# Two attention stages change places between two fences, in a hybrid encoder layer on one core

## What is computed

```python
x = x + 0.5 * SwiGLU_1(RMSNorm(x))                 # w1_gate, w1_up, w1_down; width 2816
z = RMSNorm(x) @ w_in                              # q, k, v of both groups, indexer q, k, w
# group A: differential attention, 4 heads, q/k split in two 64-wide halves
p = softmax(q1 k1) - lam * softmax(q2 k2);  o = RMSNorm(p @ v) * (1 - lam_init)
# group B (DSA): 8 heads, one shared key and value; a 4-head indexer picks
# k = min(256, L // 4) admissible keys per query, and only these are attended
x = x + concat(A, B) @ w_out
x = x + 0.5 * SwiGLU_2(RMSNorm(x))
```

## Time and profile before

| | |
|---|---|
| Timed runs | 2506.95, 2510.47, 2513.23 us; median 2510.47 |
| Profiled execution | 2504.2 us, span 2502.4 us |
| TensorE busy | 2435.7 us, 97% of the span |
| VectorE, ScalarE, GpSimd busy | 1441.7, 1044.7, 268.3 us |
| Mean granted TensorE clock | 0.995 |
| Main pieces beside the two attentions | lines 1403 to 1405 and 1420 to 1422 |

### The profile page before, as it was taken

How to read it: one execution, slowest core, us unless ns; L and a number is a source line. 1 busy time by engine, 2 the same in 40 slices (tenths; PEclk the granted TensorE clock), 3 DMA queues, 4 the chain that set the end, 5 groups by cost and what they waited for, 6 DMA issues and landing times.

```text
span 2502.4 us, 36218 instructions
## 1 busy us (share of the span) xinstructions
PE 2435.7 (97%) x13547; PEld 2104.8 (84%) x13547; DVE 1441.7 (58%) x2875; ACT 1044.7 (42%) x1811; POOL 268.3 (11%) x364
## 2 busy tenths in 40 slices
PE   7999999999999999998899999999999999999998
PEld 7999999978877678777788988999979889888887
DVE  5544444464257458887544468888875635444444
ACT  4322222233234346656433457876555533222221
POOL 1100000014210001110013200000100001000000
PEclk9999999999999999999899999999999999999999
DMA  6212121233357353333424542322321132322331
GB/s 234 81 68 85 68 85 68 85 134 110 122 163 247 113 158 123 100 115 88 175 68 148 166 146 72 101 87 73 94 61 51 37 144 84 133 93 86 102 101 67
DMA packets 169323, 271.28 MB, mean 108 GB/s; under 512 B 72032, under 2 KB 104832, under 8 KB 169152
## 3 DMA queue, kind: packets, MB, share of 16 engines
q0 software_dynamic: 43200, 167.29, 19.8%
q1 hardware_dynamic: 125952, 101.68, 12.8%
HBM read 235.21 MB, written 35.29 MB: 108 GB/s over the span
## 4 chain that ended last, share of the span: by engine, by line
PE 88%; DVE 4%; issue 3%; DMA 2%; ACT 1%; SPq 1%; DVEq 0%; POOL 0%; ACTq 0%
PE bank L1403 14%; PE bank L1405 14%; PE bank L1404 14%; PE bank L1420 7%; PE bank L1421 7%; PE bank L1422 7%; PE bank L1440 5%; PE bank L1442 5%; PE bank L1441 5%; PE bank L1532 3%; PE bank L1501 2%; PE bank L1502 1%; PE bank L1515 1%; PE bank L1460 1%; DMA rows<-o_scr 1%
## 5 line engine op out<-in xcount | busy, mean ns | idle before, releaser
L1993 DVE TENSOR_TENSOR w_lo<-raw,w_hi 128x1024 fp32r<-128x1024 f32 x320 | 385.9, 1216 | 135.4 <-ACT w_hi L1707 134.9
L1403 PE MATMUL bank<-XTh_a,w_hi 128*128 128x320 f32 x1408 | 440.4, 313 | 2.8 <-DVE w_lo L1993 2.5
L1405 PE MATMUL bank<-XTh_a,w_lo 128*128 128x320 f32 x1408 | 436.1, 310 | 0.0
L1404 PE MATMUL bank<-XTl_a,w_hi 128*128 128x320 f32 x1408 | 436.0, 310 | 0.0
L1707 ACT ACTIVATE w_hi<-raw 128x1024 fp32r<-128x1024 f32 x320 | 332.0, 1047 | 217.3 <-PE bank L1442 127.5
L1420 PE MATMUL bank<-w_hi,hid_hi 128*128 128x512 f32 x792 | 317.9, 401 | 10.9 <-DVE X_a L2024 5.4
L1421 PE MATMUL bank<-w_lo,hid_hi 128*128 128x512 f32 x792 | 312.6, 395 | 0.0
L1422 PE MATMUL bank<-w_hi,hid_lo 128*128 128x512 f32 x792 | 310.4, 392 | 0.0
L1403 PE MATMUL bank<-XTh_b,w_hi 128*128 128x512 f32 x704 | 282.8, 402 | 0.0
L2024 DVE SCALAR_TENSOR_TENSOR X_a<-bank,X_a 128x512 f32<-128x512 f32 x220 | 151.1, 689 | 224.2 <-PE bank L1422 223.5
L1404 PE MATMUL bank<-XTl_b,w_hi 128*128 128x512 f32 x704 | 278.3, 395 | 0.0
(11 more groups left out here) (326 smaller groups left out, 3954.6 us busy)
## 6 DMA issues: line engine op xcount, KB each, us to landing
raw<-in_w_gate POOLq DMA_DIRECT2D x44, 1024.0 KB, 5.6
raw<-in_w_up POOLq DMA_DIRECT2D x44, 1024.0 KB, 5.7
raw<-in_w_down POOLq DMA_DIRECT2D x44, 1024.0 KB, 5.2
raw<-in_w_in POOLq DMA_DIRECT2D x16, 1024.0 KB, 5.4
s_k_in<-in_cache_diff_k SPq DMA_DIRECT2D x16, 512.0 KB, 4.5
s_v_in<-in_cache_diff_v SPq DMA_DIRECT2D x8, 1024.0 KB, 5.9
raw<-in_w_out POOLq DMA_DIRECT2D x8, 1024.0 KB, 5.5
q_rows_b<-q_scr SPq DMA_DIRECT2D x80, 64.0 KB, 2.0
```

Source lines behind the costliest of these rows:

```text
L1403: pe.matmul(out, hi[:, k], XTh[g][:, k, lo:up], start=(k == 0), stop=False)
L1404: pe.matmul(out, hi[:, k], XTl[g][:, k, lo:up], start=False, stop=False)
L1405: last = pe.matmul(out, low[:, k], XTh[g][:, k, lo:up], start=False, stop=(k == KD - 1))
L1993: dve.tensor_tensor(hilo(w_lo, u)[:, :, 0:width_of(u)], raw_part(u), hilo(w_hi, u)[:, :, 0:width_of(u)].bitcast(F32), ALU.subtract).then_i ...
```

## The change

The two attentions of the side list change places, and `fence` with them: `enter` of GA (1) now lets the prompt's attention start, a plain raising behind `leave` (2, `past_attention`) lets the sample's start, and `past_sample` keeps its wait for the sample's stores, stands behind the sample and raises nothing. The numbers that `opened`, `near_zero` and `x_begin` wait for, and the planner's needs, are turned round to match.

```diff
@@ needs
         if kind in ("k_load", "q_load", "near", "values"):
-            return [("fence",), ("enter", GB)]
+            return [("enter", GA), ("enter", GB)]
@@
         if kind in ("x_q", "x_tables"):
-            return [("x_begin",), ("enter", GA)] + ([("x_tables",)] if kind == "x_q" else [])
+            return [("x_begin",), ("fence",)] + ([("x_tables",)] if kind == "x_q" else [])
@@ att_items
-    out += [("opened", 2 if g == GA else 3), ("k_split", g, 0), ("k_low", g, 0)]
+    out += [("opened", 1 if g == GA else 3), ("k_split", g, 0), ("k_low", g, 0)]
@@ sample_items
-    out += [("opened", 1), ("x_tables",), ("x_q", "dq"), ("x_q", "iq"), ("x_q", "w"), ("x_key", "i", 0),
+    out += [("opened", 2), ("x_tables",), ("x_q", "dq"), ("x_q", "iq"), ("x_q", "w"), ("x_key", "i", 0),
@@ make_plan
-    plan += merge(s.take(), [("enter", GA)] + sample_items() + [("fence",)] + att_items(GA)
+    plan += merge(s.take(), [("enter", GA)] + att_items(GA) + [("fence",)] + sample_items() + [("past_sample",)]
                   + [("reload", GA)] + out_items("ota", 5), pace=PACE[GA])
@@ gpsimd
                 def near_zero(g):
-                    pool.wait_ge(fence, 2 if g == GA else 3)
+                    pool.wait_ge(fence, 1 if g == GA else 3)
@@
                 def x_begin():
-                    pool.wait_ge(fence, 1)
+                    pool.wait_ge(fence, 2)
@@ sync
                 def past_sample():
                     sp.wait_ge(s_stored, 32)
+
+                def past_attention():
                     sp.sem_inc(fence, 1)
@@
-                          "fence": past_sample}
+                          "fence": past_attention, "past_sample": past_sample}
```

## The result

The changed kernel takes 2519.97 us (median of twelve runs, 2515.23 to 2523.98), the kernel before 2509.80 beside it (2505.87 to 2513.23). The ratio is 1.0043 with a 95% interval of 1.0035 to 1.0050: 10 us slower. That lies inside the forecast's range (2503 to 2526), but not at its likeliest case: +2.4 us was said, and a time over 2518 had a chance of 0.23.

What follows compares the result with a forecast made beforehand. TensorE was taken as the bound, busy 2435.7 of 2502.4 us, so only idle gaps or slow-clock stretches could change. Start 0, middle +0.5 and end +1.9 summed to +2.4 us: median 2510.47 to 2512.9, range 2503 to 2526.

Steps and rivals of the forecast that it cites:

- Start, 0: Start of the prompt's attention, now first: its loads land before the planner's some 14 pieces end; cost 0.
- Middle, +0.5: Joint from prompt's attention to sample: loads need 10.2 us against 9.7 covered by about 5 pieces; 0.5 us, bounds 0 to 4.3.
- The stages' own draw unchanged: Attention stages: each uses as many of the 217 feed-forward pieces as before; only the three joints change.
- End, stand: Sample to projection: rows ready 14.5 us after `x_end`, 4 pieces cover 5.6; TensorE stands 8.9 us at first output transpose.
- The 2.3 us of the hidden-layer chain: Tail, ahead of line 1420: this wait for the last pair goes, as the chain runs during the stand.
- End, row waits gone: Tail, third and fifth tile: the 3.0 us of row waits go, covered by four pieces behind the first transposes.
- End, clock: Tail: one slow-clock stretch losing 1.7 us follows the stand, where two of 1.7 each were lost before.
- The stock runs out: Rival: stages draw more, the 217 pieces end before `x_end`; +5 to +18 us on the forecast, 2518 to 2531; chance 0.24.
- row-wait term of 5.8 us: Part of the stock rival, in the tail: row waits of 3.0 us return, with 2.8 more for two missing pieces.
- the forecast's own case, +0.5 to +6: Whole kernel: long stand at the first output transpose, likeliest +2.4 us (2512.9); chance 0.48.
- The DSA run did not break up: Rival, DSA blocks: the planner puts pieces between them, covering up to 10 us; time 2501 to 2505; chance 0.12.
- the tail was not covered better: Rival, tail: seven or eight pieces before the first output transpose, stand 3 to 5 us; 2506.5 to 2508.5; chance 0.09.

Runs made afterwards that it cites:

- a_dx: The changed kernel with the planner's allowance for the sample's late units (dx in PACE) at 1.2 instead of 0.5; 2517.04 us, 1.0026 of the kernel before.
- b_leave0: The kernel before with the planner's landing figure for the prompt's last outputs at 0 instead of 4.0 us; 2513.10 us, ratio 1.0010.
- a_gain_dx: The changed kernel with the next norm's gain load ahead of the row loads, X_a's reloads behind them, and dx at 1.2; 2507.43 us, 0.9998 of the kernel before.
- a_gain: The changed kernel with the next norm's gain load ahead of the row loads and X_a's reloads behind them; 2515.63 us, 1.0024 of the kernel before.
- a_vwait: The changed kernel with the sample's sixth value load held back until the seventh unit's scores have begun; 2521.11 us, 1.0046 of the kernel before.

## Why the prediction was right and wrong

*Start, 0.* Right: 0.3 us of idle time in start and keys together.

*Middle, +0.5.* Right in time: no idle time in the joint, no wait at the sample's first transposes. The pieces were nine, not about five, so they covered 12.6 us, and whether the loads land within five was not put to the test. The DSA run kept its form as forecast (63.5 us, TensorE busy 80%, no feed-forward piece).

*The stages' own draw unchanged.* This step failed. The indexer and differential blocks drew 128 pieces instead of 121, and did not idle less for it. Elsewhere the draw moved too, but evened out (85 pieces against 86): the sample's own units took about six fewer, the joint four more than forecast. With the stock fixed at 217, the tail had four pieces where the forecast counted on at least eight: four ahead of the first transposes and four saved ones behind them.

*End, stand.* Right: 8.1 us against 8.9, with the four pieces ahead of it that were forecast. Its terms came as forecast too: 2.8 us from the end of the sample's transposes to the first reload, 2.4 for the reloads, 8.6 from the issue of the first row load to the first transposes, 13.8 in all against 14.5. The 2.3 us of the hidden-layer chain are gone, but not because the chain ran during this stand: it had ended under the sample, ahead of the last eight `down` pieces. In a_dx, with ten pieces left, its wait is back ahead of the stand and shortens it by about as much, so this error cost the sum nothing. An estimate by the fit of the Trainium skill, "DMA: Bandwidth & Descriptors", Anatomy of one DMA, which the prediction weighed, would make the stand 1.3 us shorter, 7.6; the trace lies between. The page gives that fit for transfers that GpSimd issues; these are SP's.

*End, row waits gone.* Wrong, and the largest miss: 5.1 us where 0 stood. The four pieces that should have come behind the first transposes were not there. a_dx shows that with six of them the waits are 0.6; b_leave0 shows, in the old order, that even then the forecast asked too much, since pieces that all stand ahead of the third tile leave the fifth uncovered.

*End, clock.* Mis-sized: one slow stretch of 1.7 us was counted. In the tail, busy PE is 14.1 us; four pieces (5.6) and forty transposes at the pace of a_gain_dx (1.91 for sixteen, 1.03 for eight: 5.0) would be 10.6, so 3.5 are lost there, and about 1.8 more in the first 3.6 us of `O`, which run at half speed.

Put together, the end costs 13.2 + 3.5 + 1.8 = 18.5 us against 8.7 before, +9.8, where the forecast had +1.9; the measured change of the medians is +10.2. That the two are so near is in part chance, for the stretch grew by 12.8 us between the two profiles. Take 1.40 us off the length for each piece, and the sample stands 5.1 us higher (112.9 against 107.8), while the 1.85 us of low clock behind the DSA blocks are gone; in a_gain and a_vwait the sample is 4.8 us shorter and the joint 3.7 us longer than in after, so that is largely one loss in two places. That the end holds the loss rests on a_gain_dx, which changes only the tail's transfers and six pieces of the sample's last units, and takes it to zero.

*The rivals.* "The stock runs out" is the case that came, in part: its row-wait term of 5.8 us was measured at 5.1, while the stand stayed at the size of the forecast, and in the sample's last 32 us TensorE idled 0.6 us, so nothing was missing there. One thing in it was off: the point from which it decides (ten pieces; seven in one stage were enough, since the row waits need only the last four). Its times, 2518 to 2531, take in the measured 2520, where the forecast's own case, +0.5 to +6, does not: the result lies in the range because that also took in the nearer half of this rival, which had been given 0.24 against 0.48. The DSA run did not break up, and the tail was not covered better.

## What to carry to other kernels

Where stages share a stock of filler work, count what a change of their order leaves for the last of them, against each single wait there: here the shortage moved to the end. When a transfer is moved back in a queue, list everything that is issued behind it and who waits for that: moving the reloads removed a stand of 8 us and made one of the same size in the projection behind. A wait that one profile shows is a suspect only; here it was removed and the time stayed.

## What was not expected of the hardware

The same instructions in the same order ran at quite different granted clocks from one kernel's execution to another's: the joint at 1.00 in after, 0.78 in a_gain and 0.78 in a_vwait, 14.4 to 18.1 us. Over the whole stretch, TensorE was busy for 503.8 to 513.1 us with practically the same work, a spread of 9 us that does not follow the idle time: a_dx was busy for 505.4 us with 32.1 idle, a_gain for 513.1 with 27.5. Differences of stages below some 5 us between two single profiles say little here; the medians decided.

A load of 0.5 MB took 16.5 us to land behind 2.6 MB of reloads and 2 MB of spills, and the row load took 6.4 us behind one such load where it took 3.3 without.
